# A decoder layer whose expert units start after a first part done for one token tile, with the rest of the first part cut into pieces between them

## The reference, cut to what matters

```python
h = x @ w_in[i]
q, k, v, gu, gv = jnp.split(h, [...], axis=-1)
attn = rms_norm(stick_breaking_attention(q, k, v), attn_out_g[i])      # causal: token t reads s < t
gm = rms_norm(gmlp_spatial_gating(gelu(gu), gelu(gv), ...), gmlp_out_g[i])   # within 128-token chunks
x = layer_norm(alpha * x + concatenate([attn, gm]) @ w_out[i], ...)
# peer: 8 heads, top 16 of 128 keys in two halves, top 16 of their 256 sums
ue = jnp.take(u_tab, idb, axis=0);  h = jnp.einsum('thkd,td->thk', ue, xb)
ve = jnp.take(v_tab, idb, axis=0);  ffn = jnp.einsum('thk,thkd->td', gates * gelu(h), ve)
x = layer_norm(alpha * x + ffn, ...)
x = layer_norm(alpha * x + sigmoid(x @ w_gate + b) * (p[i] @ w_proj), ...)
```

## Time and profile before

| | |
|---|---|
| median of 3 runs | 1673.97 us (1673.47 to 1677.72) |
| the profiled execution | 1679.83 us |
| its span, first to last instruction | 1678.0 us |
| busy: PE, DVE, ACT, POOL | 1182.8, 1062.5, 927.6, 613.7 us |
| moved by DMA | 576.60 MB |

### The profile page before, as it was taken

The page is one execution under the profiler, slowest core; times in us unless marked ns, Lnnn a source line. Parts: engine busy times, 40 slices in busy tenths (PEclk is TensorE's granted clock), DMA queues, the critical chain, the costliest instruction groups (busy, mean ns, idle before and its releaser), DMA issues.

```text
span 1678.0 us, 17689 instructions
## 1 busy us (share of the span) xinstructions
PE 1182.8 (70%) x6342; PEld 915.4 (55%) x6342; DVE 1062.5 (63%) x2442; ACT 927.6 (55%) x1571; POOL 613.7 (37%) x588
## 2 busy tenths in 40 slices
PE   8999996865866665665666665666666666668677
PEld 3444654655655555555655555555555555655453
DVE  0011246875666767677767776777676767666786
ACT  1023532764566666565656566666666656656572
POOL 0001202443344444444544454444444444443230
PEclk9999998986688778778778788777787778878899
DMA  7131015999999999999999999999999999997871
GB/s 274 58 125 50 1 51 229 373 413 417 385 395 420 421 421 421 421 421 421 420 421 420 416 413 420 421 417 413 421 421 401 420 421 421 394 422 279 321 307 38
DMA packets 80418, 576.60 MB, mean 344 GB/s; under 512 B 9157, under 2 KB 9669, under 8 KB 12490
## 3 DMA queue, kind: packets, MB, share of 16 engines
q0 software_dynamic: 73728, 536.90, 78.1%
q1 hardware_dynamic: 6602, 38.56, 6.0%
HBM read 573.33 MB, written 2.10 MB: 343 GB/s over the span
## 4 chain that ended last, share of the span: by engine, by line
PE 34%; DVE 28%; DMA 25%; ACT 7%; issue 3%; POOL 2%; DVEq 0%; SPq 0%
DMA arena<-in_uv,ids 25%; DVE arena L1026 14%; PE ps L544 9%; PE ps L380 5%; PE ps L516 5%; ACT arena L773 3%; PE ps L578 3%; PE ps L387 3%; PE ps L429 2%; POOL arena L362 2%; PE ps L490 2%; DVE arena L1038 1%; ACT actv L768 1%; PE ps L413 1%; PE ps L441 1%
## 5 line engine op out<-in xcount | busy, mean ns | idle before, releaser
L544 PE MATMUL ps<-ident,arena 128*128 128x128 f32 x4096 | 684.4, 333 | 454.7 <-ACT arena L773 454.1
L544 PEld LDWEIGHTS ps<-ident,arena 128*128 128x128 f32 x4096 | 597.5, 174 | 545.8 <-ACT arena L773 420.8
L362 POOL DMA_INDIRECT arena<-in_uv,ids x512 | 592.1, 1156 | 809.4 <-PE ps L544 692.0
L1026 DVE CUSTOM_DVE_ANT_0 arena<-arena,x 128x1024 f32<-128x1024 f32 x512 | 616.4, 1223 | 273.0 <-DMA arena<-in_uv,ids 264.6
L773 ACT ACTIVATE arena<-arena,actv 128x1024 f32<-128x1024 f32 x512 | 556.9, 1135 | 0.0
L765 ACT ACTIVATE gel<-hid 128x2 f32<-128x2 f32 x256 | 51.8, 202 | 456.9 <-DVE hid L1026 450.2
L516 PE MATMUL ps<-x1T,wq_head 128*128 128x128 f32 x1024 | 127.0, 285 | 2.0 <-ACT x1T L739 2.0
L768 ACT ACTIVATE actv<-gel,gates 128x1 f32<-128x1 f32 x512 | 123.0, 287 | 8.4
L516 PEld LDWEIGHTS ps<-x1T,wq_head 128*128 128x128 f32 x1024 | 125.5, 203 | 2.7 <-ACT x1T L739 2.6
L380 PE MATMUL ps<-arena 128*128 128x512 f32 x192 | 85.0, 605 | 6.2 <-DMA arena<-in_xT 6.2
L343 POOL TENSOR_SCALAR_AFFINE_SELECT arena<-arena 128x128 f32<-128x128 f32 x64 | 19.2, 339 | 174.5 <-DVE arena L917 169.3
(11 more groups left out here) (134 smaller groups left out, 876.5 us busy)
## 6 DMA issues: line engine op xcount, KB each, us to landing
wq_head<-in_wq SPq DMA_DIRECT2D x8, 1024.0 KB
arena<-in_uv,ids POOLq DMA_INDIRECT x512
arena<-in_w_out SPq DMA_DIRECT2D x2, 2048.0 KB, 8.0
arena<-in_w_gate SPq DMA_DIRECT2D x1, 4096.0 KB, 18.2
arena<-in_w_q SPq DMA_DIRECT2D x4, 512.0 KB, 8.9
arena<-in_xT SPq DMA_DIRECT2D x4, 512.0 KB, 6.8
arena<-in_w_k SPq DMA_DIRECT2D x1, 2048.0 KB, 14.2
arena<-in_w_v SPq DMA_DIRECT2D x1, 2048.0 KB, 8.9
```

The lines of the kernel that those rows point to most:

```text
L362: nc.gpsimd.indirect_dma_start(out=rows[:, c % RING, :], out_offset=None, in_=a["uv"][:, :], in_offset=bass.IndirectOffsetOnAxis(ap=ids[:, ...
L544: i = mm(ps[:, 2 * (t % 2) + k // 4, (k % 4) * P:(k % 4 + 1) * P], rows[:, c % RING, D + k * P:D + (k + 1) * P], ident[:, :], is_transpose ...
L1026: v.tensor_tensor_reduce(out=r, in0=r, in1=x1[:, t, :], scale=1.0, scalar=0.0, op0=ALU.mult, op1=ALU.add, accum_out=hid[:, t, c:c + 1]).th ...
```

## The change

The order of the work is replaced. Only tile 0 goes through the first part ahead of the units, and its loads come in the order in which it needs them. The units then run in the order of `UNITS`: the eight heads of tile 0, then tiles 1 to 3 in runs of one to four heads. A PSUM sum is carried over a whole run and added to the tile's accumulator at its end (`add_run`), so 12 additions stand for 32. The third field of `UNITS` names one of two buffers for query weights (the second is free only after tile 0 is stored); they are loaded 20 times instead of 8.

The rest of the first part is done in 256 steps that are the groups of the 32 units: a function `background` on PE, ACT and DVE says what each does at which step. The projections of k, q, v and gu for tiles 1 to 3 are 15 pieces in two halves each, through one PSUM bank (6); the gv projections of tiles 1 to 3 stay ahead of the units. The mixing is at steps 2, 4 and 6, the attention of tile 1 in two batches of four heads, of tiles 2 and 3 in four batches of two heads each, the output projections, norm and transposes of a tile in seven further pieces from step 40, 64 and 84. The tails of tiles 0, 2 and 1 start at steps 116, 226 and 242; that of tile 3 stays behind the last unit.

With it go some changes of form. The causal mask is added to the scores by a matmul with a constant (`neg_mask`) instead of POOL's selects. The root of a variance is taken on DVE alone, by a shift, a multiply and three Newton steps of three instructions each, instead of ACT's square root, a reciprocal and three DVE instructions. The output weights (4 MB) are loaded twice, once for tile 0 into ring slots and once more for the others. `x` is multiplied by ALPHA on ACT, the attention part of the output is scaled on DVE.

```diff
--- before.py
+++ after.py
...
+UNITS = ([(0, h, 0) for h in range(PH)]
+         + [(1, 0, 0), (1, 1, 0), (1, 2, 0), (2, 2, 0), (2, 1, 0), (2, 0, 0)]
+         + [(3, 0, 0), (3, 1, 0), (3, 2, 0), (3, 3, 0), (1, 3, 0), (2, 3, 0)]
+         + [(2, 4, 0), (1, 4, 0), (3, 4, 0), (3, 5, 0), (1, 5, 0), (2, 5, 0)]
+         + [(2, 6, 1), (2, 7, 0), (1, 7, 0), (1, 6, 1), (3, 6, 1), (3, 7, 0)])
...
+TAILS = (0, 2, 1, 3)
+TAIL_AT = {0: 116, 2: 226, 1: 242}
...
+PIECES = (("k", 0), ("k", 1), ("q", 0), ("q", 1), ("v", 1), ("k", 2), ("k", 3), ("q", 2), ("q", 3), ("v", 2), ("v", 3),
+          ("gu", 0), ("gu", 1), ("gu", 2), ("gu", 3))
+HALF_AT = ((0, 1), (2, 3), (4, 5), (6, 7), (8, 9), (10, 11), (12, 13), (15, 16), (18, 19), (20, 21), (23, 24),
+           (25, 27), (28, 30), (31, 33), (34, 36))
...
+BATCHES = ([(0, range(8)), (1, range(4)), (1, range(4, 8))]
+           + [(2, (2 * i, 2 * i + 1)) for i in range(4)] + [(3, (2 * i, 2 * i + 1)) for i in range(4)])
+Z_AT = (None, 10, 22, 43, 47, 51, 55, 63, 67, 71, 75)
+LOG_AT = (None, 12, 24, 44, 48, 52, 56, 64, 68, 72, 76)
+TILE_LAST = {0: 0, 1: 2, 2: 6, 3: 10}
+OUT_AT = {1: 40, 2: 64, 3: 84}
...
+            def load_wq(u):
+                b = UNITS[u][2]
+                if not wq_load(u)[0]:
+                    return
+                before = [v for v in range(u) if UNITS[v][2] == b]
+                if before:
+                    sp.wait_ge(q_done, before[-1] + 1)
+                else:
+                    sp.wait_ge(out_done, 2 * 16)
+                sp.dma_start(wq[b], a["wq"][UNITS[u][1]]).then_inc(wq_in[b], 16)
...
-            def gather_unit(u, t):
+            def gather_unit(u):
                 pool.wait_ge(ids_ready, u + 1)
                 for c in range(TOPK):
-                    pool.wait_ge(slot_free, u * TOPK + c + 1)
+                    if u == 0 and c == 0:
+                        pool.wait_ge(out0_done, 1)
+                    if u == 0 and c == 6:
+                        pool.wait_ge(proj_done, 8)
+                    if u * TOPK + c >= RING:
+                        pool.wait_ge(slot_free, u * TOPK + c - RING + 1)
                     nc.gpsimd.indirect_dma_start(
                         out=rows[:, c % RING, :], out_offset=None, in_=a["uv"][:, :],
-                        in_offset=bass.IndirectOffsetOnAxis(ap=ids[:, t, c:c + 1], axis=0),
+                        in_offset=bass.IndirectOffsetOnAxis(ap=ids[:, u % 4, c:c + 1], axis=0),
                     ).then_inc(rows_in[c % RING], 16)
-            for u in range(PH * NT):
...
+            for u in range(NU):
+                gather_unit(u)
...
+            pe.wait_ge(xT0_in, 16)
+            project_0(0, w_k, wk_in)
+            project_0(1, w_q, wqp_in)
...
+            def piece_half(p, half):
+                kind, b = PIECES[p]
+                if half == 0 and p:
+                    pe.wait_ge(piece_taken, p)
+                if kind == "v":
+                    i = project_tok(6, w_v, x_cols(b), 4 * half, 4 * half + 4)
+                else:
+                    w = w_k if kind == "k" else w_q if kind == "q" else w_gu
+                    for k in range(4 * half, 4 * half + 4):
+                        i = mm(ps[:, 6, 0:REST], w[:, b * D + k * P:b * D + (k + 1) * P], xT[:, k, :],
+                               start=(k == 0), stop=(k == KD - 1), skip_group_check=True)
+                if half == 1:
+                    i.then_inc(piece_done, 1)
...
+            def background(step):
+                for p in range(NP):
+                    for half in range(2):
+                        if step == HALF_AT[p][half]:
+                            piece_half(p, half)
+                for t in range(1, NT):
+                    if step == MIX_AT[t]:
+                        pe.wait_ge(mixed_kept, t)
+                        mix(t, 5)
+                for m in range(1, len(BATCHES)):
+                    if step == Z_AT[m]:
+                        open_scores(m)
+                    if step == LOG_AT[m] + 2:
+                        subtract_sums(m)
+                    if step == LOG_AT[m] + 5:
+                        weigh_values(m)
+                for t in range(1, NT):
+                    b = OUT_AT[t]
+                    if step == b:
+                        out_piece(t, 0)
+                    if step in (b + 1, b + 3, b + 4, b + 6):
+                        out_piece(t, 1 + (b + 1, b + 3, b + 4, b + 6).index(step))
+                    if step in (b + 9, b + 10):
+                        out_piece(t, step - b - 4)
+                for i in range(len(gains)):
+                    if step == 100 + 2 * i:
...
+            def combine(u, c):
+                r = RUN[u]
+                first = c == 0 and (u == 0 or RUN[u - 1] != r)
+                last = c == TOPK - 1 and u == RUN_END[r]
+                if first and r:
+                    pe.wait_ge(run_added, r if r < 3 else r - 1)
                 pe.wait_ge(scaled, u * TOPK + c + 1)
...
+            for u in range(NU):
                 for c in range(TOPK):
...
+                    if c == 12 and u + 2 < NU:
+                        key_scores(u + 2)
+                    if c % 2:
+                        background(u * NG + c // 2)
...
+                exps = [m for m in range(1, len(BATCHES)) if step == LOG_AT[m] + 4]
+                ranked = step % NG == 4 and step // NG + 1 < NU
+                if logs or exps or ranked:
+                    act.preload_act_table_set("natural_log_exp_and_others")
+                if ranked:
+                    gate_exp(step // NG + 1)
+                for m in exps:
+                    exp_args(m)
+                for m in logs:
+                    log_terms(m)
...
+            for u in range(NU):
                 for g in range(NG):
-                    dots(u, t, g)
-                    if g == 1 and last_head and t >= 2:
...
-            add_embeddings(NT - 2)
-            third_norm(NT - 2)
-            rescale(acc[:, NT - 2, :], ln3_b, out_ready)
+                            norm_gates(u + 1)
+                    background(u * NG + g)
```

More of the change, by code:

```diff
@@ new lines, in _ @@
+            i.then_inc(out0_done, 1)
+            pe.wait_ge(xT_in, 16)
+            pe.wait_ge(gv_kept, 1)
+            project_tok(2, w_gv, x_cols(1)).then_inc(proj_done, 1)
+            for j in range(2):
+                pe.wait_ge(x1_ready, j + 1)
+                transposes(j, x1[0], j).then_inc(x1T0_tr, 1)
+            pe.wait_ge(subk_in, 16)
+            query(0)
+            key_scores(0)
+            pe.wait_ge(pa0_taken, 1)
+            project_tok(3, w_gv, x_cols(2)).then_inc(proj_done, 1)
@@ new lines, in gate_product @@
+            def gate_product(i, j, k0, k1):
+                t = TAILS[i]
+                if j == 0 and k0 == 0:
+                    pe.wait_ge(tail_in, 16 * 3)
+                    pe.wait_ge(x2T_ready, 2 * i + 2)
+                for k in range(k0, k1):
+                    m = mm(ps[:, 4 + j, :], x1T[t][:, k, :], w_gate[:, k, j * HALF:(j + 1) * HALF],
+                           start=(k == 0), stop=(k == KD - 1), skip_group_check=True)
+                if k1 == KD:
+                    m.then_inc(gate_done, 1)
@@ L674, in _ @@
+            last = NT - 1
+            pe.wait_ge(run_added, NR - 1)
+            for j in range(2):
+                embedding_product(last, j, 0)
+            y_transposes(last)
+            x2_transposes(last)
+            for j in range(2):
+                gate_product(last, j, 0, KD)
         @block.scalar
@@ L859, in layer_norm_stats @@
[L859 to L867 removed]
+                var, y, w = var_e[:, 0:n], rinv[:, 0:n], rtmp[:, 0:n]
@@ L1117, in unit @@
+            for u in range(NU):
+                for g in range(NG):
+                    dots(u, g)
+                    if u and RUN[u] != RUN[u - 1] and g == (0 if RUN[u] < 3 else 1):
+                        add_run(RUN[u - 1])
+                    if u + 1 < NU:
+                        if g in (0, 1):
+                            rank_keys(u + 1, g)
+                        if g == 2:
+                            rank_sums(u + 1)
                         if g == 3:
-                            add_attn(t + 2)
@@ L1156 @@
+            add_run(NR - 1)
+            second_norm(last)
+            rescale(acc[RUN_TILE[-1]], ln2_b, x2_ready)
+            for j in range(2):
+                open_gate(last, j)
+            for j in range(2):
+                add_embedding(last, j, 0)
+            third_norm(last)
 def kernel(**inputs):
```

1427 lines of the change are left out of this document (719 added, 708 removed).

## The result

The changed kernel takes 1592.47 us (median of 4 runs, 1587.3 to 1595.54) against 1673.85 on the same chip: ratio 0.9506 [0.9476, 0.9536], 4.9% faster. In a second group of runs the same kernel took 1594.14 (0.951 [0.9492, 0.9528]). The profiled execution has a span of 1589.2 us, and the forecast's sum was a span of 1576.

The account below looks back on a forecast made before the run. Units were taken as bound by DMA bytes at 419 GB/s; 94 to first gather + 1360 bytes + 77 loss + 45 end = 1576 us span, forecast 1570 against 1673.97, range 1515 to 1640.

Parts of the forecast that it names:

- Until the first gather: Start of the kernel, tile 0's first part: first gather at 94 us instead of 266.4, bounds 85 and 105.
- Bytes: DMA traffic behind the first gather: 570.0 MB at 419 GB/s, 1360 us.
- They are worth their bytes since the share is full: In the gather stream, the 12 added reloads of query weights cost 30 us, because the DMA is full.
- Loss: DMA time lost in the units where added work no longer hides: 77 us, including start and gains.
- a unit takes its busiest engine's sum divided by a share it can reach: Rule for filled units, against 40.0 us or 42.5 with a reload; share 0.85, costing 67 us.
- the readers come a step behind: In filled units, a reason for share 0.85: new pieces are halves of 2.6 us, read a step later.
- DVE's waits for PE set the pace: All filled units run at share 0.66, DVE held at `keep_piece` and `add_piece`: loss about 300, time about 1795 us; chance 0.02.
- pieces push combines back one for one: Up to unit 12, each us of added PE work costs a us, some 200: 1709 us; chance 0.03.
- the ring hides nearly everything: In filled units, loss 49 us or less: 1543 us, or 1520 with the first gather at 85; chance 0.25.
- Dips: DMA dips in units 0 to 3, 5 and 8, deepest in 8 (15 us), with DVE waiting for PE.
- PE's clock: Filled units counted at the full 2.4 GHz, since PE's clock stood at 0.96 where it was 83% busy.
- End: From the last gather's landing to the end of the span: 45 us against 48.4 before.

Follow-up runs that it names:

- the reloads thin: Changed kernel with 18 reloads of query weights cut from 1.05 to 0.13 MB each: 1573.74 us, ratio 0.9381 to the kernel before.
- the thin projections: Changed kernel with each half of the 15 projection pieces of tiles 1 to 3 made one matmul instead of four: 1589.26 us.
- the four moves: Changed kernel with output piece first, query behind background, ACT's first gate exponential earlier, last tile's embedding product moved into unit 31: 1565.63 us.

## Why the prediction was right, and where it wasn't

**Until the first gather: 94 forecast, 98.8 measured.** The chain of waits of the kernel after, cut:

```profile
8.98 17.22 PE ps L452 x128
26.20 6.87 PE ps L459 x16
...
36.14 6.87 PE ps L459 x16
43.01 1.72 PE ps L517 x4
44.73 7.14 PE ps L452 x64
...
56.37 7.13 PE ps L552 x16
...
64.29 6.99 PE ps L552 x16
...
79.70 0.76 DVE arena L994
```

The first loads took until 8.98 instead of 7, PE's part 62.3 (8.98 to 71.3) instead of 61, DVE's 9.0 (71.48 to 80.46) instead of 9.3, and from x1 to the gather 18.3 instead of 16.8. Each step's place was right, and no load was late: behind 8.98 PE's pieces join end to end but for 2.1 us at 54.3, where three instructions of DVE stand in the chain. The k and q projections (17.2 instead of 14.2) are the largest single error: 0.27 us for a matmul of 128 columns, where the gu projection further down has 0.22 (7.14 for 32). Why the first ones are slower no run shows; the granted clock is 1.00 for both.

**Bytes: 1360 forecast, 1359 measured.** Right as a quantity, with 20 loads of query weights as forecast. Wrong as a price: "They are worth their bytes since the share is full" did not hold in units 1 and 6, where the share wasn't full. With the reloads thin, 39 us of bytes gave 20.

**Loss: 77 forecast, 83 measured, and that closeness is luck.** By place, forecast and measured: units 0 to 3 with the start 33 and 14; units 4 to 12, where the output pieces are, 22 and 50; the rest with tails and gains 22 and 19. The step that failed is "a unit takes its busiest engine's sum divided by a share it can reach", with 0.85 for all. There is no one such share. Unit 1 was PE busy for 45.5 of 46.4 us, 0.98; units 6 and 9 for 41.8 of 56.3 and 46.9 of 60.2, 0.74 and 0.78. The first carries projection halves, the others output pieces, for which DVE stood 10 us. The prediction gave as its reason that the readers come a step behind, and they do, for both kinds of piece (`keep_piece` and `add_piece` are each one step after the last half). What differs is the company: no projection half has a step with row sums or value products (steps 14, 17, 26 and 29 are left free for them), while output pieces share step 46 and 70 with a batch's row sums and 44 and 68 with the query. In unit 1 DVE stood at most 2.7 us for a projection. The rival "DVE's waits for PE set the pace" named the right place, `add_piece`, and was wrong in applying it to all filled units: two of 32 lost over 8 us. Nor is a wait of DVE a loss in itself: it stood 7.0 us for a half of v at 246.06, in unit 3, and that unit lost nothing, with the DMA at 421 GB/s, a reload beside the gathers. The rival by which pieces push combines back one for one is refuted by the thin projections (5 us for 62 us of matmuls), though the output pieces come nearer to it (23 for 31), and "the ring hides nearly everything" by the dips.

What the sum had missed is the order inside a step. It counted a batch's row sums (4.4), the query (3.7) and the piece (3.6) as work of PE to be added up; they are also a queue, at whose end DVE waits. Moving the piece to the front took 12.6 us, and the query behind it 7 to 9, with PE's sum unchanged. That is shown for some 20 us of the loss; of the 29 left in units 4 to 12 with the four moves, 14 of them in unit 9, the cause is open.

**Dips.** Forecast in units 0 to 3, 5 and 8, deepest in 8, with DVE waiting for PE. By the issue of gathers they stand in 0 and 1, 6 and 9, deepest in 9; half a unit of that is only the ring's lead. 15.2 and 22.3 us there against 5 and 15.

**PE's clock.** Counted at full in filled units. It was 1.00 in units 1 to 3 (45.5 of 46.4 and 39.1 of 39.5 us busy in the first two; 1.00 is 2.4 GHz), and 0.81, 0.85 and 0.89 in units 5, 6 and 9, where PE idled 14, 15 and 13 us. So the step held in the units that PE filled, and not in those with the output pieces; what the lower clock cost there no run separates from the waits.

**End: 45 forecast, 48 measured.** The chain of the kernel after, as the earlier trace rows:

```profile
1542.27 1.14 DVE arena L1129
...
1545.26 2.13 PE ps L755 x16
1547.39 3.44 PE ps L704 x8
...
1560.63 15.79 PE ps L696 x32
...
1585.27 0.75 DVE arena L994
```

The gate product took 15.8 instead of 14.0, with the clock at 0.81 from 1541 to the end; the first stretch, to the end of the last addition at 1549.8, took 8.8, forecast 8.3. The mechanism was right, the size 3 us off.

**In sum**, the direction, the terms and their order of size were right, the rule for the loss was wrong, and the time 22 us short, of which 5 are the first gather, 6 the loss, 3 the end, and the rest the relation of span to median (6 us below the span was assumed; here the median is 3 above it).

## What to carry to other kernels

When background work is fitted beside a stream, don't price it by the busiest engine's sum alone. For each piece ask who waits for it in order, and what stands ahead of it in its own engine's list in the same step. A reader one step later is not enough by itself: here it was for halves of 2.6 to 3.4 us that had their step nearly to themselves, in a unit with PE busy for 0.98 of the time, and not for a piece of 3.6 us behind 4.4 of row sums, in steps of 5 us. So issue first in a step what another in-order engine will block on, and last what nobody needs until the next unit. And a byte has its price where the DMA is full; the same reload was free in a unit bound by PE.

## What the hardware showed that was not expected

One core's stream of gathers of 8 KB rows held 419 or 420 GB/s in each of the eight units from 946.47 to 1279.83 us, with or without a reload beside it. Whether plain loads alone run faster is not shown: short stretches read higher, but so does a stretch with gathers, since a stretch counts each packet whole by its start. (Columns as above.)

```profile
10.00:15.00 5.00, 5.00 (x27) 5.00 (x27) 0.00 (x0) 0.00 (x0) 0.00 (x0) 1.00 1.04 434
...
698.00:708.00 10.00, 3.57 (x16) 3.27 (x16) 3.66 (x12) 2.77 (x5) 3.62 (x3) 0.81 1.04 447
```

The Trainium skill, "DMA: Bandwidth & Descriptors", section "Where 436 GB/s comes from", gives 435 GB/s as the ceiling. No slice of the profile's page comes near it (420 at most in the kernel after), and the 447 above it lasts 10 us at a share of 1.04, so these readings neither bear the figure out nor refute it; the steady 419 is 4% below.
